# A 31-tap depthwise convolution on TensorE: 128-row diagonal tiles, or four stacked channel quarters with 128x32 tap tiles

## What is computed

```python
def _causal_depthwise_conv(x, w):
    k = w.shape[0]
    return lax.conv_general_dilated(
        x, w[:, None, :], window_strides=(1,), padding=[(k - 1, 0)],
        dimension_numbers=("NWC", "WIO", "NWC"), feature_group_count=x.shape[-1])

def conformer_conv(x, w_in, w_dw, b_dw, ln_g, ln_b, w_out):
    a, gate = jnp.split(x @ w_in, 2, axis=-1)
    u = a * jax.nn.sigmoid(gate)
    u = _causal_depthwise_conv(u, w_dw) + b_dw
    u = jax.nn.silu(_layer_norm_2(u, ln_g, ln_b))
    return u @ w_out
```

## Time and profile before

| | us |
|---|---|
| median of 3 runs | 1950.65 (1943.8 to 1951.76) |
| the profiled execution | 1949.48 |
| its span | 1947.6 |
| PE busy | 1809.7 (93%) |
| DVE busy | 1473.1 (76%) |
| ACT busy | 1063.5 (55%) |
| PE's taps (L917), first to last | 518.15 to 565.93 |
| DVE's taps after the second half | 523.71 to 566.40 |

### The profile page before, as it was taken

The page is one execution under the profiler, slowest core; times in us unless marked ns, Lnnn a source line. Parts: engine busy times, 40 slices in busy tenths (PEclk is TensorE's granted clock), DMA queues, the critical chain, the costliest instruction groups (busy, mean ns, idle before and its releaser), DMA issues.

```text
span 1947.6 us, 23607 instructions
## 1 busy us (share of the span) xinstructions
PE 1809.7 (93%) x9474; PEld 1551.8 (80%) x9474; DVE 1473.1 (76%) x1313; ACT 1063.5 (55%) x913; POOL 34.2 (2%) x35
## 2 busy tenths in 40 slices
PE   0899899989988999898899999999999999999995
PEld 0788678967978998797788887888878888888884
DVE  5886656485885555567688988889888898888995
ACT  1333234463652334233576777777777677677672
POOL 0000002000000000000000000000000000000000
PEclk9999899998989999898899999999999999999998
DMA  8688243604402536444599999999999999999992
GB/s 313 234 317 322 75 171 130 216 1 162 174 1 102 194 138 237 173 173 168 211 343 355 369 351 340 343 370 355 359 345 349 373 354 345 351 364 372 358 379 100
DMA packets 206317, 505.70 MB, mean 260 GB/s; under 512 B 6698, under 2 KB 8922, under 8 KB 205186
## 3 DMA queue, kind: packets, MB, share of 16 engines
q1 hardware_dynamic: 201858, 497.60, 70.0%
q10 hardware_dynamic: 4256, 6.52, 1.1%
q0 software_dynamic: 96, 0.03, 0.0%
HBM read 503.09 MB, written 1.05 MB: 259 GB/s over the span
## 4 chain that ended last, share of the span: by engine, by line
PE 86%; DVE 8%; ACT 2%; issue 2%; ACTq 1%; POOL 1%; POOLq 0%; DVEq 0%
PE psum L661 26%; PE psum L663 26%; PE psum L662 26%; DVE R L1735 2%; PE psum L978 2%; DVE R L1483 1%; PE psum L1006 1%; POOL root_out L1378 1%; PE psum L765 1%; DVE units L1412 1%; PE psum L1047 1%; DVE stats L1795 0%; DVE x L1804 0%; ACTq L1069 0%; DVE R L1792 0%
## 5 line engine op out<-in xcount | busy, mean ns | idle before, releaser
L1412 DVE TENSOR_TENSOR units<-ring,units 128x2048 fp32r<-128x2048 f32 x451 | 1012.7, 2278 | 270.8 <-ACT units L1099 195.3
L1317 ACT CAST units<-ring 128x2048 fp32r<-128x2048 f32 x332 | 629.1, 1914 | 246.7 <-PE psum L663 141.5
L661 PE MATMUL psum<-units,xr 128*128 128x512 f32 x1120 | 443.7, 396 | 7.1 <-issue 3.6
L663 PE MATMUL psum<-units,xr 128*128 128x512 f32 x1120 | 438.8, 392 | 0.0
L662 PE MATMUL psum<-units,xr 128*128 128x512 f32 x1120 | 438.5, 392 | 0.0
L1099 ACT CAST units<-ring 128x2048 fp32r<-128x2048 f32 (+1 forms) x119 | 218.6, 1880 | 235.7 <-PE psum L663 185.2
L661 PE MATMUL psum<-units,H 128*128 128x512 f32 x696 | 275.3, 396 | 2.1 <-DVE H L1412 2.1
L662 PE MATMUL psum<-units,H 128*128 128x512 f32 x696 | 273.1, 392 | 0.0
L663 PE MATMUL psum<-units,H 128*128 128x512 f32 x696 | 272.9, 392 | 0.0
L661 PEld LDWEIGHTS psum<-units,xr 128*128 128x128 f32 x1120 | 212.0, 189 | 51.5 <-issue 6.2
L661 PE MATMUL psum<-xr,units 128*128 128x256 f32 x864 | 247.4, 286 | 1.1 <-DVE xr L1412 1.1
(11 more groups left out here) (243 smaller groups left out, 1220.4 us busy)
## 6 DMA issues: line engine op xcount, KB each, us to landing
ring<-in_moe_w_gate SPq DMA_DIRECT2D x56, 2048.0 KB, 9.5
ring<-in_moe_w_up SPq DMA_DIRECT2D x56, 2048.0 KB, 9.7
ring<-in_moe_w_down SPq DMA_DIRECT2D x56, 2048.0 KB, 9.5
ring<-in_ret_w_in SPq DMA_DIRECT2D x12, 2048.0 KB, 11.8
ring<-in_fox_w_in SPq DMA_DIRECT2D x8, 2048.0 KB, 7.7
mod_first<-in_mod_w SPq DMA_DIRECT2D x8, 1536.0 KB, 18.0
R<-in_mod_w SPq DMA_DIRECT2D x16, 768.0 KB, 6.3
ring<-in_sc_w_in SPq DMA_DIRECT2D x6, 2048.0 KB, 8.0
```

The source lines that it names most:

```text
L661: mm(dst, left[0], right[0], start=first, stop=False)
L663: return mm(dst, left[1], right[0], start=False, stop=last)
L1317: nc.scalar.copy(*expert_unit_parts(q, j, half, 0)).then_inc(unit_high, 1)
L1412: return v.tensor_tensor(dst, src, high.bitcast(F32), ALU.subtract)
```

## The change

PE now takes blocks 2 to 7 and DVE blocks 0 and 1. Of a 128-channel block, each quarter of 32 channels (`q`) is copied four times into `stacked`, one copy in each quarter of the partitions, shifted by 0, 1, 2 and 3 columns (`i`). One matmul with a 128x32 tile of tap weights then adds up four taps of 32 channels, and writes 32 partitions of the bank. Eight such steps (`j`) and four quarters make 32 matmuls of 128x32 by 256 columns for a block, 192 in all, where there were 110 of 128x128.

The copies are transfers from SBUF to SBUF that ACT starts: 16 for each pair of blocks, 48 in all, of 32 partitions x 2 blocks x 284 columns. The tap tiles of a block are one DVE product of 128x1024 (`diagonals`, L1741 of the changed kernel), in two buffers; `spread_taps` sets up its operands with 20 small copies. ACT's 110 diagonals are gone. `load_rows` moves behind the taps.

```diff
-CONV_BY_VECTOR = 5
-CONV_SHARED = 17
-DIAGS = 22
+CONV_BY_VECTOR = 2
+STACK = 4
+QUAD = P // STACK
+GROUPS = 8
+SPAN = T + STACK * (GROUPS - 1)
+DIAGS = 2
...
             wait_emptied("conf_a", 3)
-            for n, (k8, k) in enumerate(TENSOR_TAPS):
-                if k == 0:
-                    b = take_bank("conf_taps", k8)
+            for n, k8 in enumerate(CONV_BY_TENSOR):
+                b = take_bank("conf_taps", k8)
+                pe.wait_ge(stacked_in[k8 // 2], STACK * STACK * 16)
                 pe.wait_ge(diag_ready, n + 1)
-                mm(b[:, 0:T], diags[:, n % DIAGS, :], u_pad[:, k8, k:k + T], start=(k == 0), stop=block_ends(n)
-                   ).then_inc(bank_filled if block_ends(n) else diag_used, 1)
+                for j in range(GROUPS):
+                    for q in range(STACK):
+                        last = mm(b[q * QUAD:(q + 1) * QUAD, 0:T], diags[:, n % DIAGS, q * GROUPS + j, :],
+                                  stacked[:, n, q, STACK * j:STACK * j + T], start=(j == 0), stop=(j == GROUPS - 1))
+                last.then_inc(bank_filled, 1)
             for g in range(4):
                 tt, half = g // 2, g % 2
                 b = take_bank("conf_cT", g)
-                pe.wait_ge(conv_ready, 4 if half == 0 else CONV_BY_VECTOR)
-                if half == 1:
+                if half == 0:
+                    pe.wait_ge(conv_ready, CONV_BY_VECTOR)
+                    wait_emptied("conf_taps", 3)
+                else:
                     wait_emptied("conf_taps", KB - 1)
...
+            def stack(g):
+                wait_emptied("conf_a", g)
+                n = 2 * g - CONV_BY_VECTOR
+                for i in range(STACK):
+                    for q in range(STACK):
+                        act.dma_start(stacked[i * QUAD:(i + 1) * QUAD, n:n + 2, q, :],
+                                      u_pad[q * QUAD:(q + 1) * QUAD, 2 * g:2 * g + 2, i:i + SPAN]
+                                      ).then_inc(stacked_in[g], 16)
...
                 highs_until(CHUNK_AT["conf_g", c] + 2)
-                highs_until(CHUNK_AT["conf_a", c] + 2)
                 if c == 0:
-                    act.wait_ge(taps_halved, 1)
-                    for n in range(DIAGS):
-                        diagonal(n)
...
+                    highs_until(CHUNK_AT["conf_a", c] + 2)
+                    stack(1)
+            stack(2)
+            stack(3)
+            highs_until(CHUNK_AT["conf_a", 1] + 2)
+            for k8 in CONV_BY_TENSOR:
+                take_taps(k8)
+            load_rows(t["ln_mix_g_2"][0:1, :], t["ln_mix_b_2"][0:1, :])
...
+            def diagonals(n):
+                k8 = CONV_BY_TENSOR[n]
+                if n >= DIAGS:
+                    dve.wait_ge(bank_filled, BANK_AT["conf_taps", k8 - DIAGS] + 1)
+                shape = [P, STACK * GROUPS, QUAD]
+                v.tensor_tensor(diags[:, n % DIAGS], quad_ident.unsqueeze(1).to_broadcast(shape),
+                                quad_taps[:, k8].rearrange("p q j -> p (q j)").unsqueeze(2).to_broadcast(shape), ALU.mult
+                                ).then_inc(diag_ready, 1)
...
                 lows_until(CHUNK_AT["conf_a", c] + 2)
                 if c == 0:
+                    spread_taps()
+                    for n in range(DIAGS):
+                        diagonals(n)
                     for k in range(early):
                         tap(0, k)
                         tap(1, k)
             for k in range(early, TAPS):
                 tap(0, k)
                 tap(1, k)
-            for k in range(TAPS):
-                for i in range(2, CONV_BY_VECTOR):
-                    tap(i, k)
+                n = DIAGS + (k - early) // 4
+                if (k - early) % 4 == 3 and n < len(CONV_BY_TENSOR):
+                    diagonals(n)
```

More of the change, by code:

```diff
@@ L73 @@
 assert PER_EXPERT % RING == 0 and 2 * PER_EXPERT % UNITS != 1
[L76 to L82, removed]
+CONV_BY_TENSOR = list(range(CONV_BY_VECTOR, KB))
+assert STACK * GROUPS == TAPS + 1 and CONV_BY_VECTOR == 2
 V_C, V_NORM, V_CB, V_CG, V_CBETA, V_SC = 0, 1, 3, 4, 5, 6
@@ L178, in bank_plan @@
         g += [("conf_g", 2 * c + i, "A") for i in range(2)] + [("conf_a", 2 * c + i, "D") for i in range(2)]
-    g += [("conf_taps", i, "A") for i in range(CONV_BY_VECTOR - 1, KB)]
+    g += [("conf_taps", i, "A") for i in CONV_BY_TENSOR]
     g += [("conf_cT", i, "D") for i in range(4)] + [("conf_nT", i, "A") for i in range(4)]
@@ L362, in build @@
         probT = region(13824, 4, 384)
-        u_pad = region(0, KB, TAPS - 1 + T)
-        conv = region(2288, KB, T)
-        conf_n = region(4336, NT, D)
+        u_pad = region(0, KB, TAPS + T)
+        conv = region(2304, KB, T)
+        conf_n = region(4352, NT, D)
         conf_uT = split_region(0, KB, T)
@@ L369, in build @@
         conf_t = region(6400, 2, 2 * T)
-        diags = region(8448, DIAGS, P)
+        diags = region(4352, DIAGS, STACK * GROUPS, QUAD)
+        stacked = region(8448, len(CONV_BY_TENSOR), STACK, SPAN)
+        quad_ident = region(8448 + len(CONV_BY_TENSOR) * STACK * SPAN, QUAD)
+        quad_taps = gate[:, 0:KB * STACK * GROUPS].rearrange("p (k q j) -> p k q j", k=KB, q=STACK)
         rows_gb = region(11264, 2, D)
@@ L443, in build @@
         conv_ready = sem("conv_ready")
-        taps_halved = sem("taps_halved")
         diag_ready = sem("diag_ready")
-        diag_used = sem("diag_used")
+        stacked_in = {g: sem(f"stacked{g}") for g in range(CONV_BY_VECTOR // 2, KB // 2)}
         lg_ready = sem("lg_ready")
@@ L1713, in _, with spread_taps @@
             lows_until(CHUNK_AT["fox_out", 1] + 2)
[L1716 to L1720, removed]
+            v.memset(u_pad[:, :, 0:TAPS - 1], 0.0)
+            step(v.memset(u_pad[:, :, TAPS - 1 + T:], 0.0))
+            step(v.tensor_scalar(vec[:, :, V_DW:V_DW + TAPS], vec[:, :, V_DW:V_DW + TAPS], 0.5, None, ALU.mult))
+            step(v.memset(quad_taps, 0.0))
+            def spread_taps():
+                for i in range(STACK):
+                    to = slice(i * QUAD, (i + 1) * QUAD)
+                    v.tensor_copy(quad_ident[to, :], ident[to, to])
+                    for q in range(STACK):
+                        taps = vec[q * QUAD:(q + 1) * QUAD, :, V_DW + i:V_DW + TAPS:STACK]
+                        last = v.tensor_copy(quad_taps[to, :, q, 0:taps.shape[2]], taps)
+                step(last)
+            def diagonals(n):
[6 more added lines that the diff above has]
+                                ).then_inc(diag_ready, 1)
             chain = {}
             def tap(i, k):
-                if i == CONV_BY_VECTOR - 1 and k < CONV_SHARED:
-                    return
                 if k == 0:
@@ L1730, in tap @@
                 else:
[L1731 to L1734, removed]
+                    dve.wait_ge(vector_step, chain[i])
                     ins = v.scalar_tensor_tensor(conv[:, i, :], u_pad[:, i, k:k + T], vec[:, i, V_DW + k:V_DW + k + 1],
```

7 lines of the change are left out of this document (1 added, 6 removed).

## The result

| | before | after |
|---|---|---|
| median of 20 runs each | 1945.53 us (1938.72 to 1951.76) | 1953.82 us (1948.88 to 1964.28) |
| ratio after / before, with its 95% interval | | 1.0049 [1.0035, 1.0063] |
| span of the profiled execution | 1947.6 | 1951.3 |
| from the end of DVE's first-half subtractions to the statistics | 500.68 to 566.82: 66.14 | 496.58 to 569.83: 73.25 |

What follows compares the result with a forecast made beforehand. PE was taken to bound the chain (86%), with DVE and PE ending the convolution within 0.5 us of each other. Terms +18.6, +21.8 and -42.9 gave -2.5 us: 1950.65 to 1948.1 us, range 1941.5 to 1962.

Steps and rivals of the forecast that it cites:

- the price of an issue: On ACT, ahead of the casts: 0.42 us per transfer start, 13.4 for the second 32, ends 0.28 and 0.49.
- Copies and tiles ahead of the gated value: On DVE before the second half's gated values: 20 small copies 2.6 us, two tap tiles 2.4, in all 5.0.
- the tail on DVE: DVE's late 32 taps and four tiles: four rounds of 4.38 us, 17.5 to the last tile, where 106 taps took 42.5.
- The four column groups side by side: In PE's convolution matmuls: four column groups overlap fully, so a block takes 3.47 us.
- two at a time: Rival for PE's matmuls: only two column groups overlap, a block costs 6.94 us, result 1961.8; chance 0.10.
- three at a time: Rival for PE's matmuls: three column groups' worth of overlap, a block costs 4.63 us, result 1952.5; chance 0.08.
- in turn: Rival for PE's matmuls: no overlap of column groups, a block costs 13.9 us, result 1994; chance 0.05.
- some 5 us of half clock: On PE after its idle time: block 4 starts at the lower clock and costs 2.5 us more.
- queue-pushes-back case: Rival on ACT: the second 16 of the 32 issues pay 1.14 us each, 11.5 more, result 1959.6; chance 0.16.
- cheap issues: Rival on ACT: an issue costs 0.28 us, 4.5 less for the 32, result 1943.6; chance 0.09.
- issues not felt: Rival on ACT: the issues hardly cost ACT time, all 13.4 us less, result 1934.7; chance 0.03.
- sum of +18.6, +21.8 and -42.9: DVE's late taps start 18.6 us later; from there to half 1 takes 21.8 instead of 42.9: 2.5 us faster.

Runs made afterwards that it cites:

- e8: Changed kernel plus 16 small transfers on SP, four each from memory or SBUF to 32 or 128 partitions: 1962.67 us in a single run.
- e4: Changed kernel with ACT's transfers recut: blocks 2 and 3 one block each, 4 and 5 half width, 6 and 7 unchanged: 1963.51 us in a single run.
- e9: Changed kernel with blocks 4 to 7 copied by one set of 16 four-block transfers, still ahead of the casts: 1943.01 us, ratio 0.9984 to the kernel before.
- e1: Changed kernel with the next weight chunk's two casts put ahead of the second 32 transfers on ACT: 1941.7 us, ratio 0.9969 to the kernel before.
- e3: Changed kernel with the second 32 transfers issued by SP, behind its weight load, instead of ACT: 1936.31 us, ratio 0.9952 to the kernel before.
- e5: Changed kernel with the casts between the transfers for blocks 4 and 5 and those for 6 and 7: 1941.98 us, ratio 0.9991 to the kernel before.
- e10: e7 with 16 four-block transfers for blocks 4 to 7, 8 on SP and 8 on ACT: 1928.24 us, ratio 0.9906 to the kernel before.
- e7: Changed kernel: casts first, blocks 4 and 5's transfers on SP, copies and first two tiles in idle time, tiles every three taps: 1929.88 us, ratio 0.9924 to before.
- e6: Changed kernel with PE's two matmul loops swapped, so the eight steps of one quarter stand in a row: 1980.38 us in a single run.

## Why the prediction was wrong, step by step

**The step that failed** is the price of an issue: "I take 0.42, between 31 and 128; ends 0.28 and 0.49. So 32 x 0.42 = 13.4". It is 0.65 from start to start, outside both ends, and the 32 take 21.4 us (519.92 to 541.33). That is 8.0 us of the miss. The prediction had itself named issues over 0.5 as a sign of being wrong. Two errors stand in it. The value was read off a pair of transfers and multiplied by 32, though an issue that comes first or second is no sample of a long row: e8 shows 0.35, 0.44, 0.60, 0.61. And it was graded by partitions and pieces, which don't set it from 32 on (e8 for partitions; e4 and e9 for pieces). The ends of the range should have been wider for the same reason: the earlier trace rows show no more than two such issues in a row. The trace of the kernel before does have a longer row, of 128-row loads on SP at the start of the program:

```profile
3.83 3.51 SPq L600 DMA_DIRECT2D mod_first<-in_mod_w  x5
```

That is 0.70 each (0.43, 1.10, 0.77, 0.58 and 0.46), with much else in flight; it would have spoken against 0.49 as the upper end.

**Copies and tiles ahead of the gated value**: 5.0 foreseen, 6.5 measured (496.58 to 503.07). The tiles were right (2.3 for two). The copies were not: a copy of 32 partitions and 64 elements takes some 0.21 us, not 0.14, and one of 32x32 takes 0.16 to 0.18, not 0.10. I had scaled the 0.20 of a 128-element instruction, which was a reduction and no copy, with the elements, and the time hardly shrinks with them. That is 1.5 us.

**The rest of the miss**: from the cast to DVE's subtraction 2.35 instead of 2.0, and the tail on DVE 17.3 instead of 17.5, the end of PE 0.1 or 0.2 shorter. The miss is 7.1 + 2.5 = 9.6, and 8.0 + 1.5 + 0.35 - 0.2 is 9.65.

**What was right.**
- *The four column groups side by side.* 3.47 foreseen for a block; ACT takes out the last of the blocks that run without a gap at 558.32 and 561.77 and 565.22, 3.45 apart. The rivals "two at a time", "three at a time" and "in turn" fall. Against 13.9 in turn that is 4.0 times; the 13.9 is worked out from the 128x128 taps of before, and no run had it.
- The Trainium skill ("TensorE: Matmul & The Clock Gate", Part 3) has 2.38 times for three column tiles and 3.07 times for four row tiles, of 512 columns. Here four column tiles of 256 columns in fp32 give 4.0, so the trace doesn't agree with a loss of that size for this case; the measurement decides.
- *Where the path runs.* Issues, casts, subtractions, taps and tiles, last block: the chain of waits of after has just this order, and e1, e3 and e5 move it the way foreseen, by 14.4, 17.8 and 9.9 us for an expected 19, 19 and 10.4.
- *DVE's tail.* Four rounds of 4.38 foreseen, 4.30 measured (548.10, 552.40, 556.70, 561.00), with tiles of 1.22. The 42.9 us from the start of DVE's late taps to the transposes of half 1 have become 21.0 to the first transpose (548.10 to 569.13) and some 0.6 more to half 1, where 21.8 had been foreseen.
- *`load_rows`, the zero fills and the weight load* cost nothing. The load of `ffn_gate` now starts after the late subtractions, and no wait for its slot shows: from the statistics to the end it was 1380.8 us and is 1381.5.

*The clock* was near too: "some 5 us of half clock" for block 4. The windows of the changed kernel, with the columns of the earlier trace rows:

```profile
520.60:530.30 9.70, 9.69 (x128) 4.67 (x128) 0.00 (x0) 0.00 (x0) 0.00 (x0) 0.72 1.03 298
530.40:552.50 22.10, 0.00 (x0) 0.00 (x0) 8.82 (x12) 4.44 (x4) 0.00 (x0) 0.55 0.44 114
552.70:569.00 16.30, 15.92 (x256) 9.50 (x256) 12.70 (x27) 1.42 (x3) 0.00 (x0) 0.88 0.17 65
```

While PE idles the grant is 0.55 on the mean, near its lower level of 1.2 GHz; in the last four blocks it is 0.88. Block 4 lasts 5.7 us (552.63 to 558.32), which is 3.45 + 2.25, and the later ones 3.45. The prediction gave no row for its 5 us; the grant was 0.51 for the first 4.1 us of block 4 (552.6 to 556.7) and 1.00 after that. PE had caught up with DVE's tiles by the last block, so this cost nothing at the end.

**The rivals.** The queue-pushes-back case was 9.0 us slower than the kernel before (1959.6), near the 9.5 measured, but by luck, since its mechanism is not what happened: the first 16 of the 32 cost the same 0.65 as the second, of all of them only one took over a microsecond (1.16), and in the later part each transfer has landed 2.1 us after its issue began, the shortest of all 48, so no data is queued ahead of it. In the same way 1953.82 lies between 1941.5 and 1962, but that range was made for other causes and says nothing for the sum. In the earlier part the issues run beside a weight load (DMA share 1.03 from 520.6 to 530.3) at the same price. The cheap issues and the issues not felt are excluded by the 23.20 us of DVE's gap. The Trainium skill ("DMA: Bandwidth & Descriptors", Anatomy of one DMA) has about 50 ns for the dispatch by a sequencer, in its account of a transfer that GpSimd issues; on ACT and SP the runs show 0.60 to 0.65 in a long row, so that figure says nothing of this one. The same section of the Trainium skill says that many descriptors can be emitted before their added cost shows, and e4 and e9, on ACT, agree: 32, 64 and 128 pieces cost the same.

**The form of the mistake.** The chances of 0.05 below and 0.15 above left 0.80 for "within 0.5%", and with it a sum of +18.6, +21.8 and -42.9 that came to -2.5. With 32 equal issues, the error of 0.23 us in one is 7.4 us in the end, three times the forecast gain. A term that is multiplied by 32 and lies wholly on the path deserved the widest range of all.

## What to carry to other kernels

Count the issues of transfers that stand ahead of anything on an in-order engine, and price each by a long row of them, not by a pair: here 0.65 us whether it moved 36 or 145 KB. So fewer and wider transfers, another queue, or the urgent work first each gave the loss back or more (e9, e3, e1). Fewer issues help only until the data is the limit, as in e10. When an engine is relieved of work but its result is ordered behind a new burst, look at what is queued behind the burst before counting the relief; the change's own idea (four stacked quarters) took 22 us off PE's busy time in this stage, and with the four moves of e7, which lay its issues and copies beside other work, 0.8% off the program. Keep neighbouring matmuls in different column groups: the same 32 matmuls take 3.45 or 10.5 us.

## What was not expected of the hardware

- **The price of an issue depends on what stands ahead of it.** From memory to 128 partitions it is 0.35, 0.44, then 0.60 (e8); from SBUF it is 0.52 or more from the first. In a long row it stays: 0.618 each and 0.648 from start to start in the median for 32 in a row on ACT, 0.597 each on SP (e3). It doesn't depend on pieces (32, 64 or 128), or on bytes (568 or 1136 B rows, 1 to 4 blocks). Transfers of a single row are an exception, at 0.24 in a row.
- **Single issues take longer, and why is open.** Two of 0.83 to 1.16 in the changed kernel and three of 0.93 to 1.26 in e9 came while a weight load's data ran. The longest on SP in e3 (1.72, at 538.5) came 5.8 us after the weight load had landed, so that isn't the only cause.
- **Copies within SBUF fill the transfer engines at some 198 GB/s**, in pieces of 1136 B (e10, DMA share 1.04).
- **Four column groups overlap without loss** with fp32 and 256 columns, when the loop over groups is the inner one (3.45 us for a block); with it outside, little (10.5 us, e6).
- **A small copy hardly gets cheaper with its size**: on 32 partitions 0.21 to 0.22 us each from start to start for 56 or 64 elements, no faster than the 128-element instructions of the earlier trace rows.
